# Attention of a two-layer block: scores in three single PSUM banks, dense results in two, dense products whole between pairs of transposed blocks

## The chip, the cores and the metric

The kernel runs on one core of one Trainium2 chip. The metric is the device time of one execution in microseconds (us), the median of three. All data are float32.

## The reference, cut to what matters

The reference is two layers over 2048 tokens of width 1024. Only the last part of the second layer is touched by the change: attention over chosen keys, the gates, the branch projections and the output projection.

```python
s = jnp.einsum('bqgrd,bqkgd->bqgrk', qg, kg).astype(jnp.float32) * scale
s = jnp.where(valid[:, :, None, None, :], s, -jnp.inf)
p = jax.nn.softmax(s, axis=-1).astype(v.dtype)
o = jnp.einsum('bqgrk,bqkgd->bqgrd', p, vg)
...
a = dsa_attention(q, k, v, qi, ki, wi, k_sel) * jax.nn.silu(z_a)
b = multiscale_pool(u_b, pool_w[layer], pool_scale[layer]) * jax.nn.silu(z_b)
g = jax.nn.sigmoid(gates.reshape(B, S, N_BRANCHES, D_MODEL) + merge_bias[layer])
y = g[:, :, 0] * (a @ w_branch_a[layer]) + g[:, :, 1] * (b @ w_branch_b[layer])
x = x + y @ w_out[layer]
```

The kernel does not gather the chosen keys. It computes scores against all keys of a tile's past and adds a bias that is very negative where a key was not chosen.

## The kernel before, in words

The function `attention` goes over the 16 query tiles of 128 tokens in the order 4, 15, 1, 14, 3, 12, 2, 11, 5, 10, 6, 9, 7, 8, 13, 0. A tile t has (t + 1) x 128 keys, cut into blocks of up to 512, so it has 1 to 4 blocks. Each tile takes 4 steps; a step does two heads (g = 0, 1). There are 64 steps and 160 blocks in all. Five engines run programs that are written out by hand and meet at semaphores. TensorE (PE) does for each step, in this order:

1. the scores of the first two blocks of the NEXT step (`scores`, L2737), two products a block, one for each head: with two or more blocks that is a run of four products;
2. one dense product, the "first" of the step, and the values of the step before (`values`, L2762); at the start of a tile the transposed denominators (`turn_denominators`, L2770) and the values come ahead of the product;
3. the scores of the remaining blocks of the next step: for a tile of four blocks a second run of four products, for one of three blocks two products;
4. the transposes of this step's probabilities (`turn_probabilities`, L2750), 4 for a full block, with the pieces of the step's other dense products put between them.

A dense product is one seventh of a Strassen-like product of a branch (`branch`, L2799, names a1 to a7 and b1 to b7, of 8 matmuls) or of the output projection (`project`, L2815, p1 to p7, of 4 matmuls with 512 columns). Each comes in four pieces. In the last tile plain products stand in for them (L2832, L2843). The lists `DENSE`, `FIRST_DENSE` and `LAST_DENSE` give each step its names: mostly 2 to 4, one of which is the "first". A float32 matmul is two passes (two rows, "x2") in the trace; a transpose is one.

VectorE (DVE) takes the scores out of PSUM: `tensor_tensor_reduce` at L2922 adds the bias, keeps the row's extreme and counts the semaphore `masked` by one for each product. It also takes every dense result out (`take`, L2960 to L2979, and `join_heads`, L2935 and L2941) and counts `spare_taken`. ScalarE (ACT) does the exponential (L2895) and copies each transposed block out (L2901), counting `pT_taken`. GpSimd (POOL) adds and gates dense results (L2656 to L2690).

PSUM has 8 banks of 512 float32 columns in use: four for scores, as two pairs (`FRONT`), two for transposed blocks (`TURNED`), one for the values (`OUT`) and one for dense results (`SPARE`). In the last 4 steps, from `LATE_STEP` on, two banks of the scores are lent to the dense results, which then go round three. PE waits for a bank in these lines:

```python
before = j - 2 if j < LATE_BLOCK + (LATE_BLOCK % 2 == 0) else j - 1
from_one(pe, S["masked"], 2 * before + g + 1)        # scores of block j, head g
from_one(pe, S["pT_taken"], j - 1)                   # transposed block j
from_one(pe, S["spare_taken"], USES.free[name, of])  # dense product
```

The score semaphore `scores` is counted once for each block, after its second product, so DVE begins a block when both of its products are done.

Of the kernel before, what the change touches and what calls it, by code (L numbers as in the profile page):

```python
# [18 lines left out]
HEAD = 64  # L19
# [2417 lines left out]
ORDER = (4, 15, 1, 14, 3, 12, 2, 11, 5, 10, 6, 9, 7, 8, 13, 0)  # L2437
# [45 lines left out]
class Uses:  # L2483
# [4 lines left out]
    def __init__(self):  # L2488
        self.place, self.bank, self.free = {}, {}, {}
        self.loads, self.loads_of, self.last_of_load, self.loaded = [], {}, [], []  # L2490
        self.y_place = {}
        last, in_buffer, rotated = {}, [0] * RING_W, 0
        for step in range(STEPS + 1):
            n = step // PAIRS_A
            names = ([("d", n - 1)] if step % PAIRS_A == 0 and n >= 1 else []) + list(dense_of(step))
            for name, of in names:
                k = len(self.place)
                self.place[name, of] = k
                bank = rotated % 3
                rotated += step >= LATE_STEP  # L2500
                self.bank[name, of], self.free[name, of] = bank, last.get(bank, 0)
                last[bank] = k + 1
                keys = [] if name[0] in "dP" else [(name[0], 0), (name[0], 1)] if name[0] in "AB" else [(of, slot_of(name)[0])]
                for key in keys:
                    if key not in self.loads:
                        buffer = len(self.loads) % RING_W
                        in_buffer[buffer] += 32 if key[0] == "A" else 16
                        self.loads.append(key)
                        self.loaded.append(in_buffer[buffer])
                        self.last_of_load.append(0)  # L2510
                    self.last_of_load[self.loads.index(key)] = k + 1
                self.loads_of[name, of] = [self.loads.index(key) for key in keys]
                if name in ("a2", "a4", "a5", "a3") or name[0] == "A":
                    self.y_place[name, of] = len(self.y_place) + 1


USES = Uses()


def attention(nc, A, x1, stage, chosen, combined, out, KT, VC, ring, const, first_at, gates_stored):  # L2520
# [3 lines left out]
    with ExitStack() as ctx:  # L2524
        sb = lambda n, s: ctx.enter_context(nc.sbuf_tensor("at_" + n, s, F32))
        S = Signals(nc, "at")
        B = [ctx.enter_context(nc.psum_tensor(f"at_bank{i}", [P, 512], F32)) for i in range(8)]
        FRONT, TURNED, OUT, SPARE = B[0:4], B[4:6], B[6], (B[7], B[2], B[3])
        qT, bias = sb("qT", [P, 2, 4, P]), sb("bias", [P, 2, SEQ])
        za, rest = sb("za", [P, 512]), sb("rest", [P, 2, T_KT - T_BT])  # L2530
        s, pT = sb("s", [P, 2, 2, SEQ]), sb("pT", [P, 2, TILES, P])
# [8 lines left out]
        bias_of = lambda n: bias[:, n % 2, :] if n else first_at[:, 512:]  # L2540
        gate = lambda kind, e, half: rest[:, e, (512 if kind == "a" else 1536) + 512 * half:(1024 if kind == "a" else 2048) + 512 * half]
        place, y_place = USES.place, USES.y_place
        LATE_BLOCK = blocks_before(LATE_STEP)
        end_wo = lambda h, k: s[:, h, k // 3, P + 512 * (k % 3):P + 512 * (k % 3) + 512] if k < 6 else flat(pT[:, h, 4 * k - 23:4 * k - 19, :])
        front_of = lambda j: 2 * (j % 2) if j < LATE_BLOCK else 0

        def from_one(eng, sem, count):
            if count > 0:
# [2 lines left out]
        with nc.Block() as block:  # L2551
# [165 lines left out]
            def _(pe):  # L2717
                mm, tr = nc.tensor.matmul, nc.tensor.transpose

                def spare_for(name, of):  # L2720
                    from_one(pe, S["spare_taken"], USES.free[name, of])
                    bank = USES.bank[name, of]
                    if bank:
                        pe.wait_ge(S["masked"], 2 * LATE_BLOCK)
                    return SPARE[bank]

                def scores(step):
                    n, c = step // PAIRS_A, step % PAIRS_A
                    if c == 0 and n > 0:
                        pe.wait_ge(S[f"qT_loaded{n % 2}"], 16 * ((n + 1) // 2))  # L2730
                    for kb, (at, w) in enumerate(blocks(ORDER[n])):
                        j = blocks_before(step) + kb
                        before = j - 2 if j < LATE_BLOCK + (LATE_BLOCK % 2 == 0) else j - 1
                        for g in range(2):
                            from_one(pe, S["masked"], 2 * before + g + 1)
                            rows = slice(64 * g, 64 * g + 64)
                            last = mm(FRONT[front_of(j) + g][:, 0:w], qT_of(n)[rows, c, :], KT[rows, at:at + w], start=True, stop=True)  # L2737
                        last.then_inc(S["scores"], 1)
                        yield

                def turn_probabilities(step):
                    n, c = step // PAIRS_A, step % PAIRS_A
                    nb = len(blocks(ORDER[n]))
                    for g in range(2):
                        pe.wait_ge(S["probs"], 2 * step + g + 1)
                        for kb, (at, w) in enumerate(blocks(ORDER[n])):
                            j = 2 * blocks_before(step) + g * nb + kb
                            from_one(pe, S["pT_taken"], j - 1)
                            for e in range(w // P):
                                last = tr(TURNED[j % 2][:, e * P:(e + 1) * P], s[:, step % 2, g, at + e * P:at + (e + 1) * P], ident[:, :])  # L2750
                            last.then_inc(S["turned"], 1)
                            if (g * nb + kb) % 2:
                                yield

                def values(step):
# [97 lines left out]
                for step in range(-1, STEPS + 1):  # L2853
                    n, c = step // PAIRS_A, step % PAIRS_A
                    pieces = scores(step + 1) if step + 1 < STEPS else iter(())
                    names = dense_of(step) if step >= 0 else ()
                    first, others = dense(names[:1]), dense(names[1:])
                    left = 4 * len(names[1:])
                    next(pieces, None)
                    next(pieces, None)  # L2860
                    if c == 0 and 1 <= n <= TILES:
# [10 lines left out]
                    for _piece in pieces:  # L2872
                        pass
                    if 0 <= step < STEPS:
                        gaps = len(blocks(ORDER[n]))
                        for at, _turned in enumerate(turn_probabilities(step)):
                            share = -(-left // (gaps - at))
                            share = min(left, share + (share % 2 if len(names) > 2 else 0))
                            for _piece in range(share):
                                next(others, None)  # L2880
                            left -= share
                    for _piece in others:
                        pass

            @block.scalar
            def _(act):
# [17 lines left out]
            def _(dve):  # L2904
# [3 lines left out]
                def mask(step, part):  # L2908
# [8 lines left out]
                    for kb, (at, w) in list(enumerate(blocks(ORDER[n])))[2 * part:2 * part + 2]:  # L2917
                        j = blocks_before(step) + kb
                        dve.wait_ge(S["scores"], j + 1)
                        for g in range(2):  # L2920
                            least = mx[:, g, kb:kb + 1] if nb > 1 else nm[:, n % 2, 2 * c + g:2 * c + g + 1]
                            v.tensor_tensor_reduce(out=s[:, step % 2, g, at:at + w], in0=FRONT[front_of(j) + g][:, 0:w], in1=bias_of(n)[:, at:at + w], scale=HEAD ** -0.5, scalar=3.0e38,  # L2922
                                                   op0=ALU.add, op1=ALU.min, accum_out=least).then_inc(S["masked"], 1)
                    if part == 1:
                        dve.wait_ge(S["masked"], 2 * blocks_before(step + 1))
# [196 lines left out]
```

## Time and profile before

| | us |
|---|---|
| median of 3 runs (3577.97 to 3580.26) | 3579.35 |
| the profiled execution's own time | 3580.01 |
| its span, first to last instruction | 3578.2 |
| PE busy in the span | 3463.6 |
| DVE busy | 1956.2 |
| ACT busy | 1624.9 |
| start of the attention part | 2717.9 |

The attention part runs from 2717.9 us to the end, some 860 us. In a timeline a row gives the start in us, how long it took, the engine, the line, the operation with its tiles, how many instructions are merged, and in brackets the idle time ahead of it with what ended it. PE is the row of matmuls, PEld the row of their weight loads. Ends of matmuls are modelled, so the difference of two starts is the safer measure on PE.

### The profile page before, as it was taken

How to read it: one execution, taken by the hardware profiler on the slowest of the kernel's cores; microseconds unless marked ns; L12 is line 12 of the kernel's file. 1: busy time of each engine (PE TensorE's matmuls, PEld its weight loads, DVE VectorE, ACT ScalarE, POOL GpSimd, SP SyncE). 2: the span in 40 equal slices, each digit the busy share in tenths (PEclk: the TensorE clock that was granted, in tenths of full speed). 3: DMA queues.
4: the chain of work that ended last, by engine and by line, in shares of the span. 5: the costliest groups of instructions: out<-in, count | busy, mean ns of one | idle time of the engine just before them, and what ended most of it. 6: DMA issues, size and time to landing. Idle time of an engine off the chain costs nothing. (4 is left out here: it accounts for less than half of the span.)

```text
span 3578.2 us, 70731 instructions
## 1 busy us (share of the span) xinstructions
PE 3463.6 (97%) x28420; PEld 2680.8 (75%) x28420; DVE 1956.2 (55%) x4847; ACT 1624.9 (45%) x3703; POOL 704.5 (20%) x948
## 2 busy tenths in 40 slices
PE   6999999997999999989999999999999999999999
PEld 5888988885666666668787788777887677666676
DVE  5233323335777777624688778666676434444442
ACT  2222333224444444411777666877773433333340
POOL 0000000004444444310000000221110232223320
PEclk9999999997999999999999999999999999999999
DMA  9111111115122222151111114333334455555553
GB/s 312 61 48 54 54 54 54 52 66 153 71 77 77 79 88 90 59 166 59 52 55 53 53 53 163 122 110 126 107 106 176 171 200 182 215 217 218 206 184 121
DMA packets 181977, 407.93 MB, mean 114 GB/s; under 512 B 38320, under 2 KB 120256, under 8 KB 161600
## 3 DMA queue, kind: packets, MB, share of 16 engines
q1 hardware_dynamic: 173264, 394.65, 31.0%
q0 software_dynamic: 2016, 7.34, 0.5%
q8 instruction: 191, 3.13, 0.3%
q10 hardware_dynamic: 6416, 2.08, 0.2%
q14 instruction: 90, 0.74, 0.1%
HBM read 292.87 MB, written 111.15 MB: 113 GB/s over the span
## 5 line engine op out<-in xcount | busy, mean ns | idle before, releaser
L2901 ACT ACTIVATE at_pT<-at_bank 128x512 f32<-128x512 f32 (+3 forms) x320 | 154.3, 531 | 516.3 <-PE at_bank L2750 516.1
L2048 PEld LDWEIGHTS p_bank<-p_hT,w_in_rest 128*128 128x128 f32 x3072 | 345.5, 192 | 14.9 <-issue 12.4
L2048 PE MATMUL p_bank<-p_hT,w_in_rest 128*128 128x128 f32 x3072 | 350.2, 276 | 2.1 <-DVE p_st L2332 1.3
L325 PE MATMUL p_bank<-p_hT,w_in_rest 128*128 128x128 f32 x2720 | 349.2, 275 | 0.0
L325 PEld LDWEIGHTS p_bank<-p_hT,w_in_rest 128*128 128x128 f32 x2720 | 326.4, 192 | 0.0
L2169 ACT ACTIVATE p_r<-p_acc,p_mid 128x384 f32<-128x384 f32 (+13 forms) x224 | 292.9, 1308 | 60.5 <-DVE p_acc L2359 56.2
L2039 PE MATMUL p_bank<-arena,p_hT 128*128 128x512 f32 (+2 forms) x768 | 242.0, 467 | 1.3 <-ACT p_hT L2163 1.3
L2229 ACT ACTIVATE p_r<-p_bank,ahead_rows 128x512 f32<-128x512 f32 (+3 forms) x304 | 167.9, 634 | 156.0 <-PE p_bank L2142 144.0
L325 PE MATMUL p_bank<-p_hT,arena 128*128 128x128 f32 x1632 | 228.9, 276 | 4.2 <-ACT p_hT L421 2.9
L2347 DVE SCALAR_TENSOR_TENSOR p_acc<-p_r,ahead_rows,p_acc 128x512 f32<-128x512 f32 (+3 forms) x266 | 173.0, 704 | 102.4 <-ACT p_r L2229 100.0
L2130 PE MATMUL p_bank<-p_hTg,arena 128*128 128x256 f32 x1024 | 226.7, 381 | 1.7 <-ACT arena L2191 1.7
L2130 PE MATMUL p_bank<-p_hTg,w_in_rest 128*128 128x256 f32 x1024 | 228.2, 381 | 0.0
L2130 PEld LDWEIGHTS p_bank<-p_hTg,w_in_rest 128*128 128x128 f32 x1024 | 192.7, 190 | 42.0 <-issue 15.9
L2130 PEld LDWEIGHTS p_bank<-p_hTg,arena 128*128 128x128 f32 x1024 | 193.2, 190 | 39.5 <-issue 13.2
L2922 DVE CUSTOM_DVE_ANT_0 at_s<-at_bank,at_bias 128x512 f32<-128x512 f32 (+3 forms) x304 | 170.6, 613 | 94.1 <-PE at_bank L2737 91.7
L325 PEld LDWEIGHTS p_bank<-p_hT,arena 128*128 128x128 f32 x1632 | 204.7, 192 | 7.8 <-issue 4.5
L2039 PEld LDWEIGHTS p_bank<-arena,p_hT 128*128 128x128 f32 x768 | 142.4, 191 | 89.4 <-issue 69.2
L2365 DVE TENSOR_SCALAR_CACHE_REDUCE p_tie<-p_acc,p_mid 128x384 f32<-128x384 f32 (+13 forms) x126 | 186.3, 1479 | 13.8 <-ACT p_mid L2171 9.8
L2750 PEld LDWEIGHTS at_bank<-ident,at_s 128*128 128x128 f32 x1088 | 122.2, 142 | 44.6 <-issue 36.5
L2895 ACT ACTIVATE at_s<-at_s,at_nm 128x640 f32<-128x640 f32 (+15 forms) x128 | 152.5, 1199 | 3.5 <-DVE at_nm L2927 3.3
L2750 PE MATMUL at_bank<-ident,at_s 128*128 128x128 f32 x1088 | 150.3, 278 | 3.7 <-ACT at_pT L2901 3.7
L277 POOL TENSOR_TENSOR arena<-arena 128x1 f32<-128x1 f32 x16 | 3.0, 189 | 723.1 <-ACT p_xn L413 723.1
(483 smaller groups left out, 6584.9 us busy)
## 6 DMA issues: line engine op xcount, KB each, us to landing
arena<-combined SPq DMA_DIRECT2D x98, 1024.0 KB, 4.7
stage<-p_st SPq DMA_DIRECT2D x15, 1856.0 KB, 5.9
arena<-stage SPq DMA_DIRECT2D x15, 1856.0 KB, 7.5
at_rest<-stage SPq DMA_DIRECT2D x16, 1280.0 KB, 8.4
stage<-x_or_pr SPq DMA_DIRECT2D x128, 128.0 KB, 1.8
combined<-p_hT SPq DMA_DIRECT2D x16, 896.0 KB, 4.2
p_ada<-in_ada_w SPq DMA_DIRECT2D x8, 1024.0 KB, 9.2
p_xt<-in_x SPq DMA_DIRECT2D x16, 512.0 KB, 3.3
```

The lines of the kernel that those rows point to most:

```text
L325: last = mm(out, w_in(k, at, at + P), hT[:, k, 1:P + 1], start=(k == 0), stop=(k == KD - 1))
L2039: last = mm(bank[:, 0:width], hTs[:, n % 2, k, :], weights(k, c, c + width), start=(k == 0), stop=(k == KD - 1))
L2048: last = mm(bank[:, m * P:(m + 1) * P], weights(k, c + m * P, c + (m + 1) * P), hTs[:, n % 2, k, :], start=(k == 0), stop=(k == KD - 1))
L2130: last = mm(gate_bank[:, 0:2 * P], weights(k, c, c + P), hTg[:, g % 2, k, :], start=(k == 0), stop=(k == KD - 1))
L2169: ch.link(f(flat(r[:, :, :])[:, 0:L], acc[:, slot.buf_a, 0:L], ACT.Sign, scale=-1.0, bias=m, accum_out=tally[:, 0:1]))
L2229: f(r[:, q, 0:width_], FRONT[q][:, 0:width_], ACT.Relu, scale=wi[:, slot.a, head:head + 1]).then_inc(S["relu_done"], 1)
L2347: last = stt(part, r[:, q, 0:width_], sgn, part, ALU.mult, ALU.add)
L2365: ch.link(ts(tie[:, 0:L], acc[:, slot.buf_b, 0:L], m[:, 0:1], 0.0, ALU.is_ge, ALU.add, accum_out=cnt[:, 0:1]))
L2750: last = tr(TURNED[j % 2][:, e * P:(e + 1) * P], s[:, step % 2, g, at + e * P:at + (e + 1) * P], ident[:, :])
L2895: f(s[:, step % 2, g, 0:w], s[:, step % 2, g, 0:w], ACT.Exp, scale=-1.0, bias=nm[:, n % 2, h:h + 1], accum_out=den[:, n % 2, h:h + 1]).the ...
L2901: f(flat(pT[:, g, at // P:(at + wide) // P, :]), TURNED[j % 2][:, 0:wide], ACT.Copy).then_inc(S["pT_taken"], 1)
L2922: v.tensor_tensor_reduce(out=s[:, step % 2, g, at:at + w], in0=FRONT[front_of(j) + g][:, 0:w], in1=bias_of(n)[:, at:at + w], scale=HEAD ** ...
```

## The change

Three things change, all in `attention` and in the plan `Uses` that it reads.

- The scores go round three single banks: product number k = 2j + g uses bank k modulo 3, and waits until product k - 3 has been masked. Before, it waited for product k - 4, which had used the same bank of the same pair.
- The dense results go round two banks in all steps, so a product waits until the one but last before it has been taken. The special case of the last 4 steps is gone.
- The other dense products of a step are no longer spread as pieces over all gaps between pairs of transposed blocks. Each is done whole in one gap: number `at` of n products goes into gap `at * gaps // n`. For a tile of one block the two transposed blocks now have a gap between them.

```diff
-                bank = rotated % 3
-                rotated += step >= LATE_STEP
+                bank = rotated % 2
+                rotated += 1
...
-        FRONT, TURNED, OUT, SPARE = B[0:4], B[4:6], B[6], (B[7], B[2], B[3])
+        FRONT, TURNED, OUT, SPARE = B[0:3], B[4:6], B[6], (B[7], B[3])
...
-                        before = j - 2 if j < LATE_BLOCK + (LATE_BLOCK % 2 == 0) else j - 1
                         for g in range(2):
-                            from_one(pe, S["masked"], 2 * before + g + 1)
+                            from_one(pe, S["masked"], 2 * j + g - 2)
                             rows = slice(64 * g, 64 * g + 64)
-                            last = mm(FRONT[front_of(j) + g][:, 0:w], qT_of(n)[rows, c, :], KT[rows, at:at + w], start=True, stop=True)
+                            last = mm(FRONT[(2 * j + g) % 3][:, 0:w], qT_of(n)[rows, c, :], KT[rows, at:at + w], start=True, stop=True)
...
-                            if (g * nb + kb) % 2:
+                            if nb == 1 or (g * nb + kb) % 2:
                                 yield
...
-                    first, others = dense(names[:1]), dense(names[1:])
-                    left = 4 * len(names[1:])
+                    first, others = dense(names[:1]), [dense((name,)) for name in names[1:]]
...
-                        gaps = len(blocks(ORDER[n]))
-                        for at, _turned in enumerate(turn_probabilities(step)):
-                            share = -(-left // (gaps - at))
-                            share = min(left, share + (share % 2 if len(names) > 2 else 0))
-                            for _piece in range(share):
-                                next(others, None)
-                            left -= share
+                        gaps = max(2, len(blocks(ORDER[n])))
+                        for gap, _turned in enumerate(turn_probabilities(step)):
+                            for at, product in enumerate(others):
+                                if at * gaps // len(others) == gap:
+                                    for _piece in product:
+                                        pass
```

On PE, at the start of tile 12 (four blocks), the first run of scores for step 21, the transposed denominators, the values of step 19 and the dense product p6 stand like this before:

```order
L2737 MATMUL at_bank0<-KT,at_qT 128x512
L2737 MATMUL at_bank1<-KT,at_qT 128x512
L2737 MATMUL at_bank2<-KT,at_qT 128x512
L2737 MATMUL at_bank3<-KT,at_qT 128x512
L2770 MATMUL at_bank7<-ident,at_rden 128x128 x4
L2762 MATMUL at_bank6<-at_pT,VC 64x128 x8
L2815 MATMUL at_bank7<-arena,at_Sy 128x512 x4
```

And like this in the changed kernel (its line numbers are 6 lower here):

```order
L2731 MATMUL at_bank2<-KT,at_qT 128x512
L2731 MATMUL at_bank0<-KT,at_qT 128x512
L2731 MATMUL at_bank1<-KT,at_qT 128x512
L2731 MATMUL at_bank2<-KT,at_qT 128x512
L2764 MATMUL at_bank7<-ident,at_rden 128x128 x4
L2756 MATMUL at_bank6<-at_pT,VC 64x128 x8
L2809 MATMUL at_bank3<-arena,at_Sy 128x512 x4
```

The fourth score product now goes into the bank of the first, and p6 goes into another bank than the denominators, whose bank it shared before.

On PE, the transposes of that step (L2750, banks 4 and 5, two blocks a pair) with the one other dense product (L2815, p7) before:

```order
L2750 MATMUL at_bank4<-ident,at_s 128x128 x4
L2750 MATMUL at_bank5<-ident,at_s 128x128 x4
L2815 MATMUL at_bank7<-arena,at_Sy 128x512
L2750 MATMUL at_bank4<-ident,at_s 128x128 x4
L2750 MATMUL at_bank5<-ident,at_s 128x128
L2815 MATMUL at_bank7<-arena,at_Sy 128x512
L2750 MATMUL at_bank4<-ident,at_s 128x128 x4
L2750 MATMUL at_bank5<-ident,at_s 128x128 x4
L2815 MATMUL at_bank7<-arena,at_Sy 128x512
L2750 MATMUL at_bank4<-ident,at_s 128x128 x4
L2750 MATMUL at_bank5<-ident,at_s 128x128
L2815 MATMUL at_bank7<-arena,at_Sy 128x512
```

And in the changed kernel:

```order
L2744 MATMUL at_bank4<-ident,at_s 128x128 x4
L2744 MATMUL at_bank5<-ident,at_s 128x128 x4
L2809 MATMUL at_bank7<-arena,at_Sy 128x512 x4
L2744 MATMUL at_bank4<-ident,at_s 128x128 x4
L2744 MATMUL at_bank5<-ident,at_s 128x128
L2744 MATMUL at_bank4<-ident,at_s 128x128 x4
L2744 MATMUL at_bank5<-ident,at_s 128x128 x4
L2744 MATMUL at_bank4<-ident,at_s 128x128 x4
L2744 MATMUL at_bank5<-ident,at_s 128x128
```

The product stands whole behind the first pair, and the other three pairs follow each other with nothing between them.

## Rows read from the trace of the kernel before

**Rows 1.** Busy time, granted clock and DMA of stretches of the attention part

```profile
core 0: us, PE busy (x) PEld busy (x) DVE busy (x) ACT busy (x) POOL busy (x), PEclk, DMA share, GB/s
2738.00:3579.00 841.00, 814.05 (x6144) 576.19 (x6140) 341.54 (x907) 295.88 (x552) 223.19 (x206) 1.00 0.52 189
...
2785.00:2791.00 6.00, 5.15 (x36) 3.40 (x34) 2.70 (x9) 3.64 (x7) 0.00 (x0) 1.00 0.39 133
```

**Rows 2.** Groups of instructions on PE, 2717 to 3579 us

```profile
L2799 PE MATMUL at_bank<-at_T,arena 128*128 128x128 f32 x896 | 115.2, 280 | 5.1 <-DVE at_y L2970 2.5 <-DVE at_yb L2962 0.8 <-DVE at_zR L2935 0.7
...
L2815 PE MATMUL at_bank<-arena,at_Sy 128*128 128x512 f32 x224 | 107.1, 600 | 5.9 <-DVE at_zR L2935 4.1 <-DVE at_yb L2968 0.9 <-DVE at_yb L2977 0.5
L2815 PE MATMUL at_bank<-arena,at_y 128*128 128x512 f32 x168 | 77.8, 601 | 2.6 <-DVE at_y L2979 2.5
L2799 PE MATMUL at_bank<-at_rest,arena 128*128 128x128 f32 x336 | 43.5, 279 | 3.7 <-DVE at_yb L2977 3.7
L2799 PE MATMUL at_bank<-at_aT,arena 128*128 128x128 f32 x336 | 43.3, 280 | 1.6 <-DVE at_y L2960 0.8 <-DVE at_y L2977 0.7
...
L2770 PE MATMUL at_bank<-ident,at_rden 128*128 128x128 f32 x64 | 10.4, 286 | 0.4 <-DVE at_yb L2979 0.4
```

**Rows 3.** Waits of PE, 2717 to 3579 us: total us, times, longest

```profile
PE at_bank L2815 <- DVE at_zR L2935: 4.1, 5, 1.3
...
PE at_bank L2799 <- DVE at_y L2962: 0.2, 1, 0.2
```

**Rows 4.** Timeline of PE: two dense products in a row, and one unhindered

```profile
2814.28 1.95 PE L2799 MATMUL at_bank<-at_T,arena 128*128 128x128 f32 x16
2817.01 2.05 PE L2799 MATMUL at_bank<-at_T,arena 128*128 128x128 f32 x16 [0.78 <-DVE at_y L2970]
...
2885.83 1.95 PE L2799 MATMUL at_bank<-at_rest,arena 128*128 128x128 f32 x16
2887.61 0.93 PE L2750 MATMUL at_bank<-ident,at_s 128*128 128x128 f32 x7
```

**Rows 5.** Timeline: a first run of four score products, and its first mask

```profile
2951.77 1.99 PE L2737 MATMUL at_bank<-KT,at_qT 64*128 64x512 f32 x8
...
2952.30 0.19 PEld L2737 LDWEIGHTS at_bank<-KT,at_qT 64*128 64x128 f32 x2 [0.24 <-issue]
...
2952.73 0.19 PEld L2737 LDWEIGHTS at_bank<-KT,at_qT 64*128 64x128 f32 x2 [0.23 <-issue]
...
2953.09 0.69 DVE L2922 CUSTOM_DVE_ANT_0 at_s<-at_bank,at_bias 128x512 f32<-128x512 f32 x1 [0.52 <-PE at_bank L2737]
```

**Rows 6.** Timeline: PE released by a mask, at the start of the part

```profile
2719.75 0.69 DVE L2922 CUSTOM_DVE_ANT_0 at_s<-at_bank,first_at 128x512 f32<-128x512 f32 x1 [9.59 <-PE at_bank L2737]
...
2720.50 2.07 PE L2737 MATMUL at_bank<-KT,first_at 64*128 64x512 f32 x3 [0.37 <-DVE at_mx L2922]
```

**Rows 7.** Timeline: a second run of four score products, and its first mask

```profile
2959.91 1.35 PE L2737 MATMUL at_bank<-KT,at_qT 64*128 64x512 f32 x8
...
2961.08 0.69 DVE L2922 CUSTOM_DVE_ANT_0 at_s<-at_bank,at_bias 128x512 f32<-128x512 f32 x1 [0.32 <-PE at_bank L2737]
```

**Rows 8.** Timeline of PE: four pairs of transposed blocks with nothing between them

```profile
2785.77 1.09 PE L2750 MATMUL at_bank<-ident,at_s 128*128 128x128 f32 x8
2787.17 1.15 PE L2750 MATMUL at_bank<-ident,at_s 128*128 128x128 f32 x8 [0.31 <-ACT at_pT L2901]
2788.61 1.07 PE L2750 MATMUL at_bank<-ident,at_s 128*128 128x128 f32 x8 [0.29 <-ACT at_pT L2901]
2789.92 1.15 PE L2750 MATMUL at_bank<-ident,at_s 128*128 128x128 f32 x8 [0.25 <-ACT at_pT L2901]
2791.00 0.70 PE L2737 MATMUL at_bank<-KT,at_qT 64*128 64x256 f32 x4
```

**Rows 9.** Timeline of PE: a pair of transposed blocks, a piece, the next pair

```profile
2755.48 1.09 PE L2750 MATMUL at_bank<-ident,at_s 128*128 128x128 f32 x8
2756.41 0.61 PE L2799 MATMUL at_bank<-at_T,arena 128*128 128x128 f32 x4
2756.89 1.15 PE L2750 MATMUL at_bank<-ident,at_s 128*128 128x128 f32 x8
```

More of the change, by code:

```diff
@@ L2542, in attention @@
         place, y_place = USES.place, USES.y_place
-        LATE_BLOCK = blocks_before(LATE_STEP)
         end_wo = lambda h, k: s[:, h, k // 3, P + 512 * (k % 3):P + 512 * (k % 3) + 512] if k < 6 else flat(pT[:, h, 4 * k - 23:4 * k - 19, :])
-        front_of = lambda j: 2 * (j % 2) if j < LATE_BLOCK else 0
         def from_one(eng, sem, count):
@@ L2721, in spare_for @@
                     from_one(pe, S["spare_taken"], USES.free[name, of])
[L2722 to L2725, printed above, removed]
+                    return SPARE[USES.bank[name, of]]
                 def scores(step):
@@ L2874, in _ @@
                     if 0 <= step < STEPS:
-                        gaps = len(blocks(ORDER[n]))
-                        for at, _turned in enumerate(turn_probabilities(step)):
-                            share = -(-left // (gaps - at))
-                            share = min(left, share + (share % 2 if len(names) > 2 else 0))
-                            for _piece in range(share):
-                                next(others, None)
-                            left -= share
-                    for _piece in others:
-                        pass
+                        gaps = max(2, len(blocks(ORDER[n])))
[4 more added lines that the diff above has]
+                                        pass
+                    else:
+                        for product in others:
+                            for _piece in product:
+                                pass
             @block.scalar
@@ L2921, in mask @@
                             least = mx[:, g, kb:kb + 1] if nb > 1 else nm[:, n % 2, 2 * c + g:2 * c + g + 1]
-                            v.tensor_tensor_reduce(out=s[:, step % 2, g, at:at + w], in0=FRONT[front_of(j) + g][:, 0:w], in1=bias_of(n)[:, at:at + w], scale=HEAD ** -0.5, scalar=3.0e38,
+                            v.tensor_tensor_reduce(out=s[:, step % 2, g, at:at + w], in0=FRONT[(2 * j + g) % 3][:, 0:w], in1=bias_of(n)[:, at:at + w], scale=HEAD ** -0.5, scalar=3.0e38,
                                                    op0=ALU.add, op1=ALU.min, accum_out=least).then_inc(S["masked"], 1)
```

## The prediction

> **What bounds the kernel now.** I read the busy time of stretches first. From 2738 us to the end PE is busy for 814 of 841 us at a granted clock of 1.00, DVE for 342 and ACT for 296 [rows 1]. PE sets the end, and in this part nothing but work on PE or a wait of PE counts. The groups of PE's instructions tell what its idle time is ahead of: of some 24 us, 19.3 us (5.1 + 5.9 + 2.6 + 3.7 + 1.6 + 0.4) stand ahead of dense products and the denominators' transposes and end with a DVE instruction [rows 2]. The waits of PE count 35 of these; the first and the last stand there [rows 3]. That is the one bank for dense results: PE may not write it until DVE has read the last result. The timeline then gives what such a wait costs. Product a7 starts at 2814.28 and a4 at 2817.01, 2.73 us apart, where an unhindered product of the same kind lets the next start after 1.78 (2885.83 to 2887.61) [rows 4]. So the wait is 0.95 us, of which the modelled ends show 0.78: each shown wait hides 0.17 more. The product that waited also takes 2.05 in place of 1.95 us, another 0.10 for a weight load that no longer lies behind a matmul [rows 4].
>
> **Term 1, a second bank for dense results: a gain.** 19.3 us are shown; 35 waits hide 35 x 0.17 = 6.0 and restart dearer by up to 35 x 0.10 = 3.5. Waits under 0.17 us show no idle time at all; from differences of starts I estimate 2 us for them and their restarts. With two banks the result before last must have been taken, and since then a whole product, and mostly transposes or scores, have passed: at least 1.8 us against a DVE that needs 0.95. So nearly all goes: -31 us. The lower bound is the 19.3 that are shown. The first plain product of the last step waits for the joined heads, not for a bank, and is not in the sum.
>
> **Term 2, three banks for scores: a cost.** Before, the four products of a run found four banks. Now the fourth needs the bank of the first, so it needs the first mask, and this mask starts only when the first BLOCK is done, which is after the second product. The run that starts at 2951.77 has its second product at 2952.30 and its third at 2952.73, so its fourth at 2953.16, 1.39 after the start; the first mask starts at 2953.09, 1.32 after the start, and takes 0.69 [rows 5]. PE goes on 0.06 us after a mask's end (2719.75 + 0.69 to 2720.50) [rows 6]. The fourth product can start at 1.32 + 0.69 + 0.06 = 2.07 and is 0.68 us late. DVE is idle ahead of the mask in that row, so it cannot come earlier. Nothing covers the wait: what stands behind the fourth product in PE's queue, the dense product, the values and the transposes, waits with it.
>
> How many: every step of a tile with two blocks or more has such a run, 12 tiles x 4 = 48. Where the second block is narrower, the third product is shorter by 0.11 us for each 128 columns and the wait longer by as much. 36 runs have two full blocks: 36 x 0.68 = 24.5. Tiles 6, 5 and 4 have 0.78, 0.89 and 1.00: 4 x 2.67 = 10.7. The four tiles of four blocks (15, 14, 13, 12) have a second run in each step: 16 more. There the mask starts 1.17 after the start (2959.91 to 2961.08) [rows 7], where no take of DVE is ahead, and the fourth product would start at 1.39 for a full third block: waits of 0.54, 0.64, 0.75 and 0.86 us, 4 x 2.79 = 11.2. Together 46 us for 64 waits. Each also restarts PE at the 0.10 us of term 1: 6 us. No row shows this restart on a score product, so it is 0 or 6; I take 6, because the weight load there is as exposed as in [rows 4]. Term 2: +52, bounds 46 and 60 (the upper one if DVE takes a dense result of 0.69 us just ahead of a quarter of the masks).
>
> **Term 3, whole products: a cost.** Work on PE is the same. The pieces only fill the time in which ACT empties the two banks of transposed blocks. With a piece between, the next pair starts 1.41 after a pair's start and not a moment is lost: 0.93 for the pair, 0.48 for the piece [rows 9]. With nothing between it is 1.40, 1.44, 1.31 and at the end 1.08 us a pair [rows 8], so each uncovered join costs 1.40 - 0.93 = 0.47 to 0.51. Joins left uncovered: tiles of four blocks with one other product, 6 steps x 2; with two others, 4 steps x 1; tiles of three blocks with one other, 8 steps x 1. That is 24 x 0.5 = +12. Steps without other products (tile 15's last two, tile 4's first three) were uncovered before too. Bounds: 8, if narrow blocks are copied sooner, and 14. Doing pieces together saves nothing: a transpose pair and a piece cost the same in either order.
>
> **Term 4, the last four steps.** They lose a third result bank and gain a third score bank. Their blocks have 128 columns, and other work stands between their products: 0, bounds -1 and +2.
>
> **The sum.** -31 + 52 + 12 + 0 = +33. The profiled execution took 3580.0 us, so 3613; it lies 0.7 above the median of the runs, which gives 3612.5. I say 3613. For scale, 0.2% is 7 us, about what a measurement of this kernel tells from no change.
>
> **Two rules weighed.** In the rows, one result bank costs PE 0.95 us a time, and a fourth score product after three banks would be 0.68 late. The Trainium skill (Perfetto Trace Analysis, Matmuls) says that independent matmul groups should rotate through different banks, so that emptying one overlaps the next group. For the dense results the trace agrees, and by that rule alone both rings would be deep enough: term 2 would be 0 and the time 3561. This is rival B.
>
> In the rows, 32 transposes in a row with waits between run at a granted clock of 1.00, PE busy for 5.15 of 6 us [rows 1]. The Trainium skill (TensorE: Matmul & The Clock Gate, Part 4: PE-mode transpose) says that transposes don't count as activity for the clock. By it the longer bare runs of transposes could cost the full clock, rival C; this trace does not agree so far.
>
> **The rivals.**
> A, the forecast above: 3613, chance 0.74. Its own range is 3603 to 3621, from the bounds -31 + 46 + 8 = +23 and -25 + 52 + 14 = +41 (25 is what the shown waits and their hidden part make).
> B, faster: the wait for the first mask is covered. It would need masks that start after the first product, or PE with other work queued there. The count of `scores` comes after the second product and PE keeps its order, so the rows speak against it. The wait per run decides: under (31 - 12) / 64 = 0.30 us the change gains; at zero it is 3580 - 31 + 12 = 3561. Chance 0.06, with 0.04 more for something between that ends within 0.2%.
> C, the clock falls: in each of the 16 steps of tiles with four blocks, which wait twice for masks and mostly have bare pairs, PE drops to 1.2 GHz for some 3 us and does half of the work in them. That is 16 x 1.5 = 24 us more, 3637. Against it stands the 1.00 in [rows 1]. Chance 0.06.
> D, inputs become late: with its bank free a dense product waits for DVE's and POOL's sums (`T_ready`, `Sy_ready`, `y_added`). DVE and POOL are busy for 342 and 223 of 841 us [rows 1] and the change leaves their order alone, but each mask and each take is now a link closer to PE. If 10 of term 1's 31 us come back so: 3623. Chance 0.10.
>
> **How the numbers follow.** A, C and D are slower: 0.90. B splits into faster 0.06 and same 0.04. The range from 3598 to 3627 holds A and D whole, a little below for a smaller term 2, and leaves out B and C's upper part, under 2 in 10.
>
> **What would show it.** Right: PE has 64 waits at the scores' line ended by DVE's mask, 0.5 to 0.8 us each as shown; waits of dense products for DVE's takes are gone but for the last step's first product; waits of transposes for ACT's copies appear at up to 24 more places, 0.25 to 0.31 us each as shown; clock 1.00; DVE's and ACT's busy time the same. Wrong: if no waits at the scores' line show, term 2 fails and B holds; if dense products wait for POOL, D; if the granted clock is under 1.00 after bare transposes, C. The sum is most exposed to term 2: it counts on one wait of a known size 64 times, so 0.1 us in it moves the end by 6.

## The result, and the profile after

The changed kernel takes 3637.95 us (median of four, 3635.77 to 3639.89) against 3579.26 beside it: ratio 1.0168, 95% interval 1.0155 to 1.018, 58.7 us slower. Forecast were 3613 us and a range from 3598 to 3627. The direction was right, the size was not.

The chain's bound is the same: PE sets the end. The windows view of the attention part answers to the first row of [rows 1]: 59 us longer at the same granted clock of 1.00, with 58 us more of PE "busy", though PE has no more work (28420 matmul rows in either trace).

```profile
core 0: us, PE busy (x) PEld busy (x) DVE busy (x) ACT busy (x) POOL busy (x), PEclk, DMA share, GB/s
2738.00:3638.00 900.00, 872.09 (x6182) 596.33 (x6179) 348.24 (x916) 299.76 (x558) 222.78 (x206) 1.00 0.50 176
```

All waits of PE in the part (total us, times, longest). The waits for dense results, of which [rows 3] shows two, are gone but for the one for the joined heads in the last step. New are waits for masks, and waits for ACT's copies are three times as many (9 before).

```profile
PE at_bank L2744 <- ACT at_pT L2895: 10.8, 27, 0.7
PE at_bank L2731 <- DVE at_mx L2916: 10.3, 24, 0.9
PE at_bank L2731 <- PEq L51: 3.1, 1, 3.1
PE at_bank L2826 <- DVE at_aT L2935: 1.3, 1, 1.3
```

(The 3.1 us for PE's own sequencer stand in before too.)

Ahead of 2738 us the clock is not the same. At the start of the part PE waits in both kernels and the granted clock falls to its lower level, 0.50; here is the stretch behind, of before and of the changed kernel:

```profile
2728.00:2738.00 10.00, 8.53 (x80) 5.74 (x80) 3.78 (x18) 5.88 (x17) 2.92 (x4) 0.97 1.01 423
2728.00:2738.00 10.00, 8.85 (x42) 5.87 (x39) 1.98 (x9) 3.88 (x11) 2.88 (x4) 0.50 1.01 427
```

The changed kernel stays at 0.50 for these 10 us. What that costs is read further down, beside e10.

The table of waits shows 24 of the 64 mask waits. The groups by shape show where the others are. Of before, the score products by width (busy us, mean ns | idle ahead):

```profile
L2737 PE MATMUL at_bank<-KT,at_qT 64*128 64x512 f32 x432 | 111.1, 622 | 0.0
L2737 PE MATMUL at_bank<-KT,at_qT 64*128 64x384 f32 x64 | 13.8, 508 | 0.0
L2737 PE MATMUL at_bank<-KT,at_qT 64*128 64x256 f32 x64 | 10.4, 402 | 0.0
```

Of after, one kind of dense product that idled in [rows 2], then the same groups and their weight loads:

```profile
L2809 PE MATMUL at_bank<-arena,at_Sy 128*128 128x512 f32 x224 | 102.1, 598 | 0.0
...
L2731 PE MATMUL at_bank<-KT,at_qT 64*128 64x512 f32 x432 | 155.5, 631 | 3.2
...
L2731 PEld LDWEIGHTS at_bank<-KT,at_qT 64*128 64x128 f32 x608 | 67.8, 185 | 103.3 <-DVE at_mx L2916 52.8 <-issue 48.6
...
L2731 PE MATMUL at_bank<-KT,at_qT 64*128 64x384 f32 x64 | 21.0, 522 | 1.9 <-DVE at_mx L2916 1.9
L2731 PE MATMUL at_bank<-KT,at_qT 64*128 64x256 f32 x64 | 15.9, 415 | 3.6 <-DVE at_mx L2916 3.6
```

The same number of passes of the same shapes, each modelled some 10 ns longer, covers 44.4 + 7.2 + 5.5 = 57 us more. Mean duration times count is far more than the busy time in either kernel (432 x 0.622 = 269 against 111 before, 432 x 0.631 = 273 against 155.5 after), so passes lie over each other, and now less than before. The timeline of one run shows how. Two rows of before that [rows 5] leaves out, the first weight loads of its run and what stands behind it:

```profile
2951.77 0.30 PEld L2737 LDWEIGHTS at_bank<-KT,at_qT 64*128 64x128 f32 x4 [0.76 <-issue]
...
2953.69 0.66 PE L2770 MATMUL at_bank<-ident,at_rden 128*128 128x128 f32 x4
```

And the run of the changed kernel that answers to it:

```profile
2973.50 0.30 PEld L2731 LDWEIGHTS at_bank<-KT,at_qT 64*128 64x128 f32 x4 [0.17 <-issue]
2973.51 3.19 PE L2731 MATMUL at_bank<-KT,at_qT 64*128 64x512 f32 x8
...
2974.04 0.19 PEld L2731 LDWEIGHTS at_bank<-KT,at_qT 64*128 64x128 f32 x1 [0.24 <-issue]
...
2974.47 0.19 PEld L2731 LDWEIGHTS at_bank<-KT,at_qT 64*128 64x128 f32 x1 [0.24 <-issue]
2974.82 0.69 DVE L2916 CUSTOM_DVE_ANT_0 at_s<-at_bank,at_bias 128x512 f32<-128x512 f32 x1 [0.95 <-PE at_bank L2731]
...
2975.57 0.29 PEld L2731 LDWEIGHTS at_bank<-KT,at_qT 64*128 64x128 f32 x2 [0.92 <-DVE at_mx L2916]
...
2976.63 0.66 PE L2764 MATMUL at_bank<-ident,at_rden 128*128 128x128 f32 x4
```

The first mask starts 1.31 us after the run and the fourth product 2.07 after it, at 2975.57, both as forecast. But what stands behind the run starts at 2976.63, 1.06 after the fourth product, where the forecast had 0.53 (2953.16, its start of the fourth in before, to 2953.69, where the denominators start). And the weight loads tell what else changed: x4, x2, x2 before, x4, x1, x1, x2 now. Before, both heads' loads of a pass come together; now those of the second block come one at a time. The run takes 3.13 us in place of 1.92: 0.68 of wait and 0.53 behind it, where the forecast had 0.10.

### The profile page after: what moved, and what is told of

Same layout as the page of the kernel before. It is cut to its first block and busy times, and to the rows that moved or that the text cites. A ratio compares the mean times of both kernels' runs of the same rounds, so it can differ in the third digit from the quotient of the medians.

```text
span 3637.0 us, 70728 instructions
## 1 busy us (share of the span) xinstructions
PE 3521.4 (97%) x28420; PEld 2701.0 (74%) x28420; DVE 1959.8 (54%) x4847; ACT 1626.4 (45%) x3703; POOL 702.8 (19%) x948
## 3 DMA queue, kind: packets, MB, share of 16 engines
q8 instruction: 191, 3.13, 0.4%
## 5 line engine op out<-in xcount | busy, mean ns | idle before, releaser
L2731 PE MATMUL at_bank<-KT,at_qT 64*128 64x512 f32 (+3 forms) x608 | 196.6, 572 | 11.0 <-DVE at_mx L2916 7.8
```

What stands on the lines that cost most here:

```text
L2731: last = mm(FRONT[(2 * j + g) % 3][:, 0:w], qT_of(n)[rows, c, :], KT[rows, at:at + w], start=True, stop=True)
```

## The experiments

Each ratio is to the kernel before, timed beside it on the same chip; before took 3577.64 us for e1 to e4, 3577.15 for e5 to e8 and 3578.47 for e9 and e10, against 3579.26 beside the changed kernel. "Stalls" below are sums over the starts of PE in the trace, beyond the plain spacing of each kind of work.

### The three parts apart

e1: the kernel before with three single score banks, one result bank (in the last steps too), pieces.

```diff
-        FRONT, TURNED, OUT, SPARE = B[0:4], B[4:6], B[6], (B[7], B[2], B[3])
+        FRONT, TURNED, OUT, SPARE = B[0:3], B[4:6], B[6], (B[7],)
...
-                            from_one(pe, S["masked"], 2 * before + g + 1)
+                            from_one(pe, S["masked"], 2 * j + g - 2)
```

> The kernel before with the scores round three single banks and nothing else of the change: one bank for dense results in all steps, pieces spread as before. Theory O (overlap): the two heads' products of a block use different halves of the array's rows and run at the same time, 0.86 us for the two; the late fourth product loses this, so a run costs 0.68 us of wait plus 0.53 us. 64 runs: 46 + 28 = +74 us over the kernel before, and 0 to 4 for the last steps, which have one result bank here: 3653 to 3657. Theory R (restart): any wait of PE for a semaphore costs a fixed 0.5 us on top: the same 3653 to 3657. The forecast's own term 2 (46 + 6): 3631.

Measured: 3659.42 us (1.0225, 1.0208 to 1.0242), 81.8 over before.

e2: the changed kernel with the dense products in pieces as before (the old loop over `share`).

> The changed kernel with both rings of banks, but the dense products spread as pieces as before. Both theories: the uncovered joins of transposed blocks go, 15 us less than the changed kernel: 3622. If the whole products cost what the forecast's term 3 said: 3626. If they cost nothing: 3638.

Measured: 3624.61 us (1.0131, 1.0114 to 1.0148). e1 and e2 differ by the second result bank alone: 34.8 us. e2 and the changed kernel differ by whole products alone: 13.3 us, or 11.7 if each is first set against the before beside it.

e3: the kernel before with whole products alone.

```diff
-                            for _piece in range(share):
-                                next(others, None)
+                                if at * gaps // len(others) == gap:
+                                    for _piece in product:
+                                        pass
```

> The kernel before with its banks, and only the dense products done whole. The uncovered joins cost 15 us; products that stood close together with one result bank now have a pair of transposed blocks between them, which may save up to 8 us of their waits: 3587, between 3583 and 3595. If the whole products also spare PE something of their own: under 3579.

Measured: 3587.22 us (1.0025, 1.0015 to 1.0036), 9.6 over before. Its waits for ACT's copies are those of the changed kernel (27, 10.9 us); the dense waits shrink, from 18.6 us shown to 15.7.

So terms 1 and 3 hold, and the miss is in the scores: e1 costs 82 where 52 was forecast.

### What the fourth product costs

Two theories. O (overlap): a score product has 64 rows, and the two heads' products of a block lie on the two halves of TensorE's rows and run at the same time, 0.86 us for both at 512 columns (two passes of 0.43). If the second must wait for a mask, the first runs alone and the second runs alone behind it, and the pair costs twice. R (restart): each product takes its own 0.43 in turn, and a wait costs PE a fixed 0.5 us to get going again.

e4: the changed kernel, waiting for both banks of a block ahead of its first product.

```diff
+                        from_one(pe, S["masked"], 2 * j - 1)
                         for g in range(2):
-                            from_one(pe, S["masked"], 2 * j + g - 2)
```

> The changed kernel, but PE waits for the bank of a block's second product ahead of its first, so that both heads' products always start together; the third product of a run waits 1.1 us in place of 0.68 for the fourth. Theory O: the pair then takes 0.86 us together where the two took 0.43 + 1.05 us with the wait between; the end of a run stays where it was, 3636 to 3641. Theory R: the wait costs its 0.5 us all the same, and the run ends 0.34 us later: 64 x 0.34 = 22 more, 3660.

Measured: 3637.34 us (1.0167, 1.015 to 1.0184), the changed kernel's own time, though the third product now starts 1.1 us later. Its waits and one run of its timeline:

```profile
PE at_bank L2731 <- DVE at_mx L2916: 57.4, 64, 0.9
```

```profile
2969.34 1.13 PE L2731 MATMUL at_bank<-KT,at_qT 64*128 64x512 f32 x4
...
2971.41 0.30 PEld L2731 LDWEIGHTS at_bank<-KT,at_qT 64*128 64x128 f32 x4 [1.77 <-DVE at_mx L2916]
2971.41 1.13 PE L2731 MATMUL at_bank<-KT,at_qT 64*128 64x512 f32 x4 [0.94 <-DVE at_mx L2916]
...
2972.47 0.42 PEld L2764 LDWEIGHTS at_bank<-ident,at_rden 128*128 128x128 f32 x4 [0.76 <-issue]
```

Both products of the second block start 2.07 us after the run and are done 1.06 later: two products together take as long as the fourth alone takes in the changed kernel. That is O. R would have added the third product's time to each run. All 64 waits are shown now, since no lone product's modelled passes lie over them.

e5: before, with the order of a run changed to head 0 of both blocks, then head 1 of both.

```diff
-                    for kb, (at, w) in enumerate(blocks(ORDER[n])):
-                        j = blocks_before(step) + kb
+                    for low in range(0, len(cut), 2):
                         for g in range(2):
+                            for kb, (at, w) in list(enumerate(cut))[low:low + 2]:
```

> The kernel before with all its banks and no new wait: only the order within a run of four score products changes, from block 0 head 0, block 0 head 1, block 1 head 0, block 1 head 1 to both blocks of head 0 first and then both of head 1. Theory O (two heads of a block use different halves of the array's rows and overlap when they stand next to each other): only the middle two overlap, a run takes 0.86 us longer, 64 x 0.86 = 55 us: 3633, between 3625 and 3640. Theory R (a product takes 0.43 us by itself, and the changed kernel pays for the restart after a wait): no change, 3578.

Measured: 3589.74 us (1.0035, 1.0022 to 1.0048), near neither number. The overlap was not lost, though another product stands between the two of a block:

```profile
2953.71 0.31 PEld L2739 LDWEIGHTS at_bank<-KT,at_qT 64*128 64x128 f32 x4 [0.76 <-issue]
2953.71 1.99 PE L2739 MATMUL at_bank<-KT,at_qT 64*128 64x512 f32 x8
...
2955.63 0.42 PEld L2774 LDWEIGHTS at_bank<-ident,at_rden 128*128 128x128 f32 x4 [0.76 <-issue]
...
2955.88 0.69 DVE L2926 CUSTOM_DVE_ANT_0 at_s<-at_bank,at_bias 128x512 f32<-128x512 f32 x1 [1.37 <-PE at_bank L2739]
```

The run takes 1.92 us as before. My theory O had it that only neighbours pair up; that fell. Of the 12 us these rows show another cause: the count of the first block reaches DVE only at the end of the run, so the first mask starts 2.17 after the run's start, not 1.32. Yet the pass that carries this count starts 0.55 after the run's start, as in before (0.54): as these rows have it, the third product of the queue runs early beside the first, but its count waits for the second, which ends with the run. The takes behind the masks in DVE's queue are later by as much. PE's waits for one of them, that of the transposed denominators (`at_zR`, in `join_heads`), grow from 4.1 us in 5 [rows 3] to 9.2 in 6, and ahead of the branch's products from 0.7 to 2.7:

```profile
PE at_bank L2819 <- DVE at_zR L2939: 9.2, 6, 2.2
```

That is 7.1 us. Another 1.7 are clock: behind one of these waits, 1.98 us long, the granted clock is 0.50 from 3064.5 to 3067.9 us, and the product there takes 5.32 us to the next start in place of 3.63. The rest, some 3 us, stays open.

e9: before, with head 1's score products left out from step 8 on. This leaves out half of the score work there, and its time is read for that alone.

```diff
-                        for g in range(2):
+                        for g in range(2 if step < 8 else 1):
```

> The kernel before without the second head's score products from step 8 on (136 blocks; DVE masks whatever stands in those banks, so half of the scores are left out; all else is done). It measures what the second head's product costs PE when it stands next to the first's. Theory O (the two run at the same time on two halves of the array's rows): a block of one head takes as long as one of two, 0.86 us if full, and the time stays: 3578, between 3572 and 3583. Theory R (each takes its 0.43 us in turn): 136 blocks x 0.38 us on average less, 3526.

Measured: 3577.54 us (0.9998, 0.9988 to 1.0007). No change at all. Of e9, the score groups from 2737 to 3575 us:

```profile
L2737 PE MATMUL at_bank<-KT,at_qT 64*128 64x512 f32 x240 | 108.7, 621 | 0.0
...
L2737 PE MATMUL at_bank<-KT,at_qT 64*128 64x384 f32 x32 | 13.7, 508 | 0.0
L2737 PE MATMUL at_bank<-KT,at_qT 64*128 64x256 f32 x32 | 10.3, 402 | 0.0
```

A little over half of the products (the first 8 steps have both heads) fill nearly the same time as all of them in before (x432, 111.1; x64, 13.8; x64, 10.4). The second head's product is free as long as it may start with the first. This is the plainest proof of O.

e10: the changed kernel, with `scores` counted after each product, so the mask of a block's first product need not wait for the second.

```diff
-                        last.then_inc(S["scores"], 1)
+                            last.then_inc(S["scores"], 1)
...
-                        dve.wait_ge(S["scores"], j + 1)
                         for g in range(2):
+                            dve.wait_ge(S["scores"], 2 * j + g + 1)
```

> The changed kernel with the semaphore of the scores counted once for each product, so that the first mask may start when the first product is done and not when its block is. Theory O: both products of the first block end together, so the mask starts no sooner: as the changed kernel, 3634 to 3642. Theory R: the first product is done 0.43 us before the second, the fourth waits that much less: 64 x 0.43 = 27 less, 3611.

Measured: 3631.57 us (1.0149, 1.0132 to 1.0166), 6 under the changed kernel, whose interval (1.0155 to 1.018) it meets. Under R the first product would be done 0.4 us before the second and the mask would start that much sooner. It does not (a run's start at 2966.47, the mask, and the weight load of the fourth product):

```profile
2966.47 3.17 PE L2731 MATMUL at_bank<-KT,at_qT 64*128 64x512 f32 x8
...
2967.77 0.69 DVE L2916 CUSTOM_DVE_ANT_0 at_s<-at_bank,at_bias 128x512 f32<-128x512 f32 x1 [0.94 <-PE at_bank L2731]
...
2968.53 0.29 PEld L2731 LDWEIGHTS at_bank<-KT,at_qT 64*128 64x128 f32 x2 [0.90 <-DVE at_mx L2916]
```

Mask after 1.30 us, fourth product after 2.06: the two products of a block end together. The second block's first mask does start sooner, since it no longer waits for the late fourth product (2.53 after the run's start, in the changed kernel 3.24, 2973.50 to 2976.74), but that is not where most of the 6 us are. Set start against start, the traced e10 is 7.7 us ahead of the traced changed kernel at the end of the part and already 6.7 ahead at 2743 us. Half of this is the clock. e10's is 1.00 from 2728 to 2738 us, where the changed kernel's is 0.50:

```profile
2728.00:2738.00 10.00, 7.82 (x64) 5.05 (x59) 2.15 (x10) 5.46 (x15) 2.11 (x3) 1.00 1.02 428
```

From its second stretch of scores to its fourth e10 takes 12.7 us (2723.74 to 2736.44) and the changed kernel 16.1 (2727.07 to 2743.18): 3.4 us for 10 us more at the lower clock. Executions of one kernel differ in the clock, too: e4's two with a mean granted clock of 0.992 took 3632.79 and 3634.84 us, its two with 0.988 and 0.989 took 3639.85 and 3641.5. e10's four had 0.991 and 0.992, the changed kernel's four 0.988 to 0.991. So some 3 to 4 us are left for the counting; which of PE's starts they come from stays open.

### Runs cut apart

With three banks one block can always be in flight, so a second block should find its banks if other work stands between. e6 has both rings and pieces, with a block, the first dense product, a block, the values, a block, the first transposed pair, a block (at a tile's start: a block, denominators and values, a block, the first product, a block).

```diff
                     next(pieces, None)
-                    next(pieces, None)
                     if c == 0 and 1 <= n <= TILES:
...
                         for _piece in first:
                             pass
+                        next(pieces, None)
                         if 0 <= step - 1 < STEPS:
                             values(step - 1)
-                    for _piece in pieces:
-                        pass
+                    next(pieces, None)
...
                         for at, _turned in enumerate(turn_probabilities(step)):
+                            next(pieces, None)
```

> Three score banks, two result banks, pieces as before, but no run of four score products is left: the second block's two products stand behind the first dense product (at a tile's start behind the values), the third block's behind the values, the fourth block's behind the first pair of transposed blocks. The first mask is then done before the fourth product comes. Theory O: 74 us of waits and lost overlap go and the second result bank keeps its gain of 27 to 30 us; a few more changes between kinds of matmul cost 3 to 6: 3553, between 3548 and 3558. If the second bank had gained little and the whole products did it: 3575 to 3580.

Measured: 3568.23 us (0.9975, 0.9966 to 0.9984). It beats both kernels, before by 8.9 us and the changed one by 68 (each against its own before), and falls 15 short of what I expected. Mask waits are down to 3.0 us and dense waits are gone:

```profile
PE at_bank L2744 <- ACT at_pT L2898: 3.5, 8, 0.7
PE at_bank L2731 <- DVE at_mx L2919: 3.0, 4, 0.9
PE at_bank L2826 <- DVE at_aT L2938: 1.4, 1, 1.4
```

What eats most of the gain is the switch between 64-row and 128-row work. A lone block of e6:

```profile
2935.83 0.30 PEld L2731 LDWEIGHTS at_bank<-KT,at_qT 64*128 64x128 f32 x4 [0.76 <-issue]
2935.83 1.13 PE L2731 MATMUL at_bank<-KT,at_qT 64*128 64x512 f32 x4
2936.89 3.70 PE L2809 MATMUL at_bank<-arena,at_y 128*128 128x512 f32 x8
```

It takes 1.06 us to the next start, two of them 2.12, where two in a run take 1.92 (2951.77 to 2953.69): 0.20 for each cut. 64 cuts make 13 of the 15 us, an estimate from this one figure. Before shows one side of it as well: the second pass of a dense product with 512 columns starts 0.53 after the first where scores stand ahead (all 14 times), and mostly 0.43 where transposes do.

e7: the kernel before with e6's order alone.

> The kernel before with its four score banks and one result bank, only the order of scores as in e6. It tells the gain of the second result bank from that of the order: if the order alone is worth nothing, 3580 to 3584 (3 to 6 us for changes between kinds of matmul).

Measured: 3620.7 us (1.0123, 1.0108 to 1.0139), 43.6 slower, a clear miss. I had counted the switches and not the one result bank:

```profile
PE at_bank L2815 <- DVE at_zR L2938: 12.1, 6, 2.0
PE at_bank L2799 <- DVE at_zR L2938: 9.3, 5, 2.0
```

These two waits add 16.6 us to the 4.1 + 0.7 of before [rows 2, 3], and the stalls between a block of scores and the dense product right behind it rise from 0.9 to 26.9 us. Why they grow stands in the timeline. DVE takes the transposed denominators behind the masks of the first two blocks, and the second block's products now come after the values:

```profile
2962.90 1.13 PE L2737 MATMUL at_bank<-KT,at_qT 64*128 64x512 f32 x4
2964.08 0.69 DVE L2925 CUSTOM_DVE_ANT_0 at_s<-at_bank,at_bias 128x512 f32<-128x512 f32 x1 [1.22 <-PE at_bank L2737]
...
2965.31 0.68 DVE L2938 TENSOR_TENSOR at_zR<-at_bank,at_za 128x512 f32<-128x512 f32 x1
2966.05 5.40 PE L2815 MATMUL at_bank<-arena,at_Sy 128*128 128x512 f32 x8 [2.01 <-DVE at_zR L2938]
```

In before this take starts 3.76 us after the run of scores (2951.77 to 2955.53), in e7 5.08 after the first block (2960.23 to 2965.31), and the product behind it waits 2.01 in place of 0.91 us. The last row shows one thing more: the product takes 5.40 us, where the same 8 passes take 3.60 to 3.70 elsewhere, at half the clock:

```profile
2966.85:2970.20 3.35, 3.35 (x5) 1.35 (x4) 0.00 (x0) 0.00 (x0) 0.00 (x0) 0.50 0.00 0
```

This happens three times in e7 (from 2850.80, 2966.85 and 3297.95 us), each time behind a wait of 2.0 us, and costs 3 x 1.7 = 5 us; other waits of 2.0 us were not followed by it. With 13 for the cuts that makes 35 of the 44 us. The same order costs 44 us on before's banks; on the two rings it gains 56 against the old order (e2 to e6).

e8: e6 with whole products.

> As e6, with the dense products whole as in the changed kernel. The uncovered joins cost some 15 us, less 2 to 4 where the fourth block's scores now stand in one of them: 3565, between 3560 and 3570.

Measured: 3582.9 us (1.0015, 1.0006 to 1.0024). The miss is e6's 15 us again, and 3 more for whole products, which cost 14.7 us here, 13.3 in the changed kernel and 9.6 in before.

## Why the prediction was wrong

**The step that failed is the price of a run in term 2**: "Each also restarts PE at the 0.10 us of term 1: 6 us." The wait came out: the fourth product starts 2.07 after the run, and is late by 0.68, 0.78, 0.89 and 1.04 us against the forecast's own start for the four widths of the second block (forecast 1.00 for the last) and by 0.54 to 0.86 in second runs, 46 us in all. But behind the wait the fourth product then takes 1.06 us at 512 columns, not 0.53 and a restart. It no longer runs beside the third. The excess is one pass of its width and the restart: 0.43 + 0.10 = 0.53 at 512 columns, 0.43 at 384, 0.32 at 256, 0.22 at 128. Over the 64 runs: 36 x 0.53 + 4 x 0.97 + 4 x 1.50 = 29 us, where the forecast had 6. Term 2 as counted is then 46 + 29 = 75, over its upper bound of 60, and 3613 + 23 = 3636 against 3638 measured. The traces bear the 75 out: the 64 runs, each from its start to that of the work behind it, take 75 us longer in the changed kernel than in before. (The bound of 60 was itself added up short: 52 and 16 x 0.69 are 63.) The longer stretch at the lower clock ahead of 2738 us, 3.4 us in the traced execution, is in no term; about 1 of it lies in those 75.

e1, with the same waits and one result bank, costs 82. It shows 41 dense waits of 22.2 us where before has 36 of 20.0, with what they hide (5 x 0.27) some 4 us. Its clock stays low longer too, 0.72 from 2728 to 2738 us, and it loses 1.9 us there against e10; 1 us stays open.

The timeline of [rows 5] could have told it: the weight loads come as x4, x2, x2, and 8 passes take 1.92 us where 8 passes of a dense product take 3.43 (2985.15 to 2988.58, below), 0.43 each. I took the spacing of 0.43 to 0.53 for the time of one product. It is one pass of both heads. So 2952.30 is the second pass of the first block, the third and the fourth product start together at 2952.73, and 2953.16 is their second pass. Against that true start of 0.97 the fourth is 1.10 late, not 0.68. That the parts still add up is in part luck: the start of 2.07 hangs on the mask alone, which was read from the trace, and the sum needs only that start and the end of the run. The same rows also show the restart that the prediction missed on scores: 0.53 to the second pass, 0.43 after.

The Trainium skill (TensorE: Matmul & The Clock Gate, Part 3: Packing small matmuls — row/col tiling) says that matmuls on different row groups of the array run concurrently, started within 4 ns of each other. The trace agrees that they run side by side, with starts 7 ns apart: in before, passes of the two heads start at 2951.770 and .777, 2952.303 and .310. That rule spoke against this change, and the forecast did not weigh it. In the changed kernel the first block's passes start as pairs, 0 and .007, .533 and .540 us after the run's start; the third product's start alone, at 0.962 and 1.392, and the fourth's alone, at 2.07 and 2.60.

**Term 1 (second result bank), -31: right.** The waits are gone and the group's idle time is 0.0. e1 to e2 gives -34.8, of which some 4 are the waits that e1 has beyond before's; against before that leaves about 31. No run took the second bank alone on before's four score banks.

**Term 3 (whole products), +12: right.** 11.7 to 13.3 between e2 and the changed kernel. Stalls between transposes, from 2738 us on, rise from 6.5 to 20.6 us. The wait for ACT is 27 times against 9, so 18 of the 24 joins show it, 0.25 us behind a full pair of 8 transposes and 0.67 behind one of 5, which gives ACT less time:

```profile
2985.15 3.60 PE L2809 MATMUL at_bank<-arena,at_Sy 128*128 128x512 f32 x8
2988.58 0.71 PE L2744 MATMUL at_bank<-ident,at_s 128*128 128x128 f32 x5
2989.96 1.06 PE L2744 MATMUL at_bank<-ident,at_s 128*128 128x128 f32 x8 [0.67 <-ACT at_pT L2895]
2991.28 0.82 PE L2744 MATMUL at_bank<-ident,at_s 128*128 128x128 f32 x5 [0.25 <-ACT at_pT L2895]
```

**Term 4, 0:** no row of the last steps speaks against it, and no run measured it by itself.

**The signs named.** "64 waits at the scores' line" failed as a sign: 24 are shown, since the third product's lone passes are modelled over the wait. The weight loads' idle time for masks (52.8 us) was the place to look. The rest came as named: dense waits gone, ACT's waits at 18 more places, clock 1.00 from 2738 us on, DVE's and ACT's busy time over the whole span the same within 4 us (1956.2 and 1959.8, 1624.9 and 1626.4).

**The rivals.** B fell: the mask wait is not covered. C gives 3637 us, as measured, for the wrong reason: in the steps that it names the granted clock is 1.00, though PE stands still there for up to 0.9 us at a time. What it fears did happen elsewhere, in e7 and e5 behind waits of 2.0 us, at 1.7 us a time (its 1.5 stood on no row). In the changed kernel's longest bare runs of transposes, 32 in a row from 2811.53 to 2816.76 us, the granted clock is 1.00. The Trainium skill (TensorE: Matmul & The Clock Gate, Part 4: PE-mode transpose), by which transposes don't count as activity for the clock, is not borne out by them. D fell: no wait of PE ends with POOL.

## What to carry to other kernels

Products on half of TensorE's rows that run side by side are one unit of work: size the ring of PSUM banks in whole pairs, or else let the wait stand where other work covers it, because a wait between the two costs as much as one ahead of both: behind it the late one takes the pair's whole time (e4). Before pricing a stretch of short products, divide its time by its work: if a row's products fill less than their passes should take, they overlap, and whatever separates them gives that back. An order and a ring belong together: the cut order lost 44 us on one pair of rings and gained 56 on the other. And look at the granted clock of every stretch before explaining a few us: 6 us between e10 and the changed kernel were mostly at the start of the part, half of them clock.

## What the runs showed of the hardware

- Half of the score products left out, from step 8 on, changed nothing: 3577.54 us against 3578.47 (0.9988 to 1.0007), so the second half-row float32 product costs no time beside the first.
- The two need not be neighbours in the queue: with another product between them the run still took 1.92 us (e5). But the count of the later one came 0.85 us later than when they were neighbours, though its last pass started at the same 0.55 us.
- A block of 64-row products between 128-row work costs 0.20 us more than the same block in a run (1.06 each against 1.92 for two).
- Two products that overlap end together: counted apart, the first let its mask start at 1.30 us, against 1.31 for both.
- Behind a wait of 2.0 us of PE the granted clock fell to 0.50 three times in e7 and once in e5, not behind every such wait, and 8 passes of 512 columns took 5.3 us to the next start in place of 3.63; waits of up to 0.9 us in the changed kernel left it at 1.00.
